# Odd layer's attention: the memory branch runs first, and the compressed branch is computed for all heads between its steps

## The chip, the core and the metric

One NeuronCore of a Trainium2 chip runs the whole program. Its engines have queues of their own: TensorE (PE; its weight loads stand as PEld), VectorE (DVE), ScalarE (ACT), GpSimd (POOL) and SyncE (SP), which here only issues DMAs. They meet at semaphores. TensorE writes to the eight banks of PSUM (`ps`), 128 partitions by 512 fp32 numbers each. The metric is the time of one launch on the device in microseconds (us). All numbers are fp32; one fp32 matmul of this kernel appears in the trace as two MATMUL instructions, a transpose as one.

## What is computed

Two blocks in a row on 512 tokens of width 1024. The change lies in one stage of the odd layer of the first block. That layer's attention, cut to what matters:

```python
def block(s0):                       # queries s0 .. of 12 heads, 2 groups of keys
    sc = jnp.einsum('bghqd,bgjd->bghqj', qb, kcmp) + head_bias(rel_c)      # 31 compressed keys
    pc = masked_softmax(sc, rel_c >= 0) * (tpos >= CMP_BLOCK - 1)...
    oc = jnp.einsum('bghqj,bgjd->bghqd', pc, vcmp)
    ...                              # selected blocks: all 8 blocks of 64 keys are selected
    ps = masked_softmax(ss, (rel_s >= 0)[:, :, None])
    osel = jnp.einsum('bghqk,bgqkd->bghqd', ps, vg)
    ...
    ow = jnp.einsum('bghqk,bgkd->bghqd', pw, vwb)                          # window of 512 keys
    return gb[:, 0, ..., None] * oc + gb[:, 1, ..., None] * osel + gb[:, 2, ..., None] * ow

def odd_layer(...):
    c = nsa_attention(q, kc, vc, ks, vs, kw, vw, gl, ...)
    m = mem_attention(xq, mem_n, w_mem_kv)                                 # 4 heads, 256 memory rows
    y = jnp.concatenate([c, m], axis=-1) * jax.nn.silu(gate)
    return h + (y @ w_out).astype(h.dtype)
```

So a head's output is a gated sum of three branches (compressed, selected, window), and beside the 12 heads stand 4 heads of attention over the memory. Everything goes into `y`, which already holds the gate.

## The kernel before

The program is a list of stages (`STAGES`). After each one `end_phase` (L202) joins all engines at a barrier, so nothing of one stage overlaps the next. The stage of this case is `nsa` (L1455). `compress` (L1351) ahead of it makes the 31 compressed keys `k.kcmpT` and values `k.vcmp` and writes the position bias, one row of 2048 numbers for each head, to `k.bias_dram`. `odd_out` (`out_projection`, L1179) follows it; its first DMA issues (L404, L1205) wait for the barrier.

Queries are in 4 tiles of 128. `nsa` has three parts, one after the other:

1. **The compressed softmax of all heads and tiles** (the prelude). SyncE issues 32 DMAs of bias into `pc` (L1487). TensorE makes the scores, 48 matmuls of a 128-column weight tile on 31 keys (L1502), a head to a bank. VectorE waits for all 32 DMAs and adds them (L1575, one head at a time), then handles all 1488 numbers of a partition at once: minimum (L1579), subtraction (L1585), sum (L1587), gate over sum (L1588, L1589), product (L1590); ScalarE's exponential (L1550) stands between. Scores are negated, so the minimum is the softmax's maximum.
2. **The main loop**, 48 steps (12 heads by 4 tiles t, head by head) in a software pipeline. A tile t has (t + 1) x 128 keys. At iteration u TensorE makes two score banks of step u, selected and window (L1513), then the products of step u-3 (L1524, then the compressed one, L1526), then transposes of step u-2: the compressed weights (L1535), then the two branches (L1541). VectorE adds the bias and takes the minimum of step u (L1601, a custom instruction and its small accumulator read), copies the transposed weights of step u-2 out of PSUM (L1610 the compressed 31 rows, L1612 the window branch) and finishes step u-3 (L1617 to L1628: two small ones, then selected, window and compressed product added up in `acc`, then times `y`). ScalarE takes the exponentials of step u (L1559) and copies the selected branch's transposed weights of step u-2 (L1567). Scores alternate between banks 0, 1 and 2, 3, transposes use banks 4 and 5, products banks 6 and 7.
3. **The memory branch**, `MemAttention` (L915): 16 steps (4 heads by 4 tiles) pipelined likewise. A step is one score matmul (L936), two transposes (L944), two product matmuls (L954) on TensorE; minimum (L975), copy (L981), reciprocal (L987) and scaling (L989) on VectorE; one exponential (L965) on ScalarE. It uses banks 0 to 5 and starts when the main loop's last result is stored.

`k.link` makes VectorE wait for its own instruction to end before the next starts. The order on each engine is the order in which the code issues; no scheduler moves anything.

## Time and profile before

| what | value |
|---|---|
| median of 3 runs | 2745.45 us (2738.14 to 2745.59) |
| the profiled execution | 2748.92 us, its span 2747.0 us |
| TensorE busy, of the span | 2320.9 us, 84% |
| VectorE, ScalarE busy | 823.9 us, 457.9 us |
| `nsa`, first instruction to last | 858.9 to 1099.0 us of the span |

The profiled execution took 3.5 us more than the median, and 1.9 us lie outside its span. In the rows further down a time is counted from the start of the span. The granted clock is the share of TensorE's full 2.4 GHz: 1.00 is 2.4 GHz, 0.50 is 1.2 GHz. A duration in the timeline includes the tail of an instruction, so neighbours on one engine overlap a little; start to start is what an instruction takes in a row of them. A row "x4" is four of a kind in a row, with the time from the first one's start to the last one's end.

### The profile page before, as it was taken

Reading aid. Unit: us, or ns where it says so; the run is one execution under the profiler, and the core shown is the slowest. Engines: PE = TensorE matmul, PEld = TensorE weight load, DVE = VectorE, ACT = ScalarE, POOL = GpSimd, SP = SyncE. Lnnn points to the kernel's source line nnn. Section 1 sums busy time; section 2 is a strip of 40 time slices with the busy share of each in tenths; the row PEclk is TensorE's granted clock in tenths of the full one; section 3 lists DMA queues with packets and bytes.
Section 4 is the critical chain, followed back from the end, with each engine's and each line's share of the span. In section 5 each row is a group of like instructions: output and inputs, shape, how many; then the busy total and the mean of one; then the engine's idle time right before and its main releaser. Section 6 shows DMA issues by size and latency. Waiting matters only on the chain. (4 is left out here: it accounts for less than half of the span.)

```text
span 2747.0 us, 32370 instructions
## 1 busy us (share of the span) xinstructions
PE 2320.9 (84%) x13640; PEld 1728.8 (63%) x13640; DVE 823.9 (30%) x1709; ACT 457.9 (17%) x791; POOL 165.7 (6%) x108
## 2 busy tenths in 40 slices
PE   7999978799976998959947993998989989898882
PEld 5788767678865777748844443656555666566651
DVE  6353164233211787433251215111111111111102
ACT  2222213121310443231201003000000000000001
POOL 0710000000000000730000001000000000000001
PEclk9999999899985999989978996999999999999996
DMA  9443203223332000425162142799999999999994
GB/s 280 140 133 97 72 1 128 88 92 93 106 117 52 17 20 5 168 78 164 59 139 94 61 167 92 320 425 426 426 426 425 427 425 426 425 426 426 426 426 152
DMA packets 148149, 581.70 MB, mean 212 GB/s; under 512 B 34678, under 2 KB 56950, under 8 KB 114038
## 3 DMA queue, kind: packets, MB, share of 16 engines
q1 hardware_dynamic: 143027, 558.59, 52.9%
q0 software_dynamic: 3824, 16.81, 1.7%
q10 hardware_dynamic: 1152, 4.19, 0.4%
q8 instruction: 111, 1.82, 0.3%
q14 instruction: 35, 0.29, 0.0%
HBM read 541.93 MB, written 37.63 MB: 211 GB/s over the span
## 5 line engine op out<-in xcount | busy, mean ns | idle before, releaser
L447 PE MATMUL ps<-w_parts,u_parts 128*128 128x512 f32 (+3 forms) x2016 | 424.2, 372 | 10.1 <-DVE w_parts L416 10.1
L2369 PE MATMUL ps<-mem,mem_u 128*64 128x256 f32 x2880 | 364.4, 409 | 72.9 <-DMA mem<-in_expert_w_gate 70.6
L447 PEld LDWEIGHTS ps<-w_parts,u_parts 128*128 128x128 f32 x2016 | 364.1, 190 | 67.6 <-issue 11.2
L2369 PEld LDWEIGHTS ps<-mem,mem_u 128*64 128x64 f32 x2880 | 254.6, 148 | 181.0 <-issue 93.2
L416 DVE TENSOR_TENSOR w_parts<-w_raw,w_parts 128x2048 fp32r<-128x2048 f32 (+3 forms) x76 | 172.8, 2275 | 407.9 <-ACT w_parts L411 407.9
L2452 DVE TENSOR_TENSOR mem_c<-mem_c,ps 128x256 f32<-128x256 f32 x64 | 26.9, 421 | 763.2 <-issue 702.0
L411 ACT CAST w_parts<-w_raw 128x2048 fp32r<-128x2048 f32 (+3 forms) x76 | 134.8, 1776 | 470.8 <-PE ps L447 209.2
L445 PE MATMUL ps<-u_parts,w_parts 128*128 128x512 f32 x768 | 177.2, 392 | 3.1 <-DVE w_parts L416 3.1
L2369 PE MATMUL ps<-mem_u 128*64 128x256 f32 x1216 | 153.3, 409 | 29.6 <-DMA mem_u<-in_expert_w_gate 28.8
L1227 PE MATMUL ps<-w_parts,u_parts 128*128 128x512 f32 x768 | 175.4, 390 | 0.0
L2382 PE MATMUL ps<-mem,mem_c 128*64 128x512 f32 x736 | 166.8, 592 | 0.5 <-DVE mem_c L2458 0.5
L445 PEld LDWEIGHTS ps<-u_parts,w_parts 128*128 128x128 f32 x768 | 145.2, 189 | 33.5 <-issue 3.4
L1227 PEld LDWEIGHTS ps<-w_parts,u_parts 128*128 128x128 f32 x768 | 144.7, 189 | 29.9
L2361 PE MATMUL ps<-picks,hn_parts 128*128 128x256 f32 x1024 | 140.4, 291 | 19.0 <-DVE picks L2432 19.0
L2361 PEld LDWEIGHTS ps<-picks,hn_parts 128*128 128x128 f32 x1024 | 127.6, 193 | 42.3 <-issue 23.1
L2369 PEld LDWEIGHTS ps<-mem_u 128*64 128x64 f32 x1216 | 106.1, 148 | 75.9 <-issue 39.6
L2422 ACT ACTIVATE mem_c<-ps 128x256 f32<-128x256 f32 x64 | 24.5, 383 | 721.6 <-PE ps L2369 721.6
L2382 PEld LDWEIGHTS ps<-mem,mem_c 128*64 128x64 f32 x736 | 61.2, 137 | 77.6 <-issue 72.5
L2440 DVE COPY mem_u<-ps 128x512 f32<-128x512 f32 x64 | 44.2, 691 | 104.3 <-PE ps L2361 104.3
L1524 PEld LDWEIGHTS ps<-mem_u 128*128 128x128 f32 x480 | 59.0, 191 | 25.6 <-ACT mem_u L1567 14.4
L1524 PE MATMUL ps<-mem_u 128*128 128x128 f32 x480 | 63.5, 279 | 11.4 <-ACT mem_u L1567 9.6
L2416 ACT COPY mem_u<-ps 128x512 f32<-128x512 f32 x64 | 37.5, 585 | 200.3 <-PE ps L2382 200.3
(335 smaller groups left out, 2309.9 us busy)
## 6 DMA issues: line engine op xcount, KB each, us to landing
mem<-in_expert_w_down SPq DMA_DIRECT2D x46, 2048.0 KB, 29.2
mem<-in_expert_w_gate SPq DMA_DIRECT2D x45, 2048.0 KB, 22.4
mem<-in_expert_w_up SPq DMA_DIRECT2D x45, 2048.0 KB, 26.9
mem_u<-in_expert_w_gate SPq DMA_DIRECT2D x19, 2048.0 KB, 22.8
mem_u<-in_expert_w_up SPq DMA_DIRECT2D x19, 2048.0 KB, 27.9
mem_u<-in_expert_w_down SPq DMA_DIRECT2D x18, 2048.0 KB, 29.7
w_raw<-in_od_w_in SPq DMA_DIRECT2D x18, 1024.0 KB, 5.1
ypad<-mem_u SPq DMA_DIRECT2D x128, 128.0 KB, 26.4
```

The costliest lines, as they stand in the source:

```text
L411: act.copy(self.part(n, 0), self.raw(n)).then_inc(self.high, 1)
L416: dve.tensor_tensor(self.part(n, 1), self.raw(n), self.part(n, 0).bitcast(F32), ALU.subtract).then_inc(self.low, 1)
L445: mm = pe.matmul(out, w[x][:, kk, g.t * P:(g.t + 1) * P], u[:, y, ku, :], start=first, stop=last)
L447: mm = pe.matmul(out, u[:, x, ku, g.t * P:(g.t + 1) * P], w[y][:, kk, :], start=first, stop=last)
L1227: mm = pe.matmul(k.ps[:, g.bank, :], parts[g.part // 2][:, x, ky, g.t * P:(g.t + 1) * P], w[z][:, kk, :], start=g.part == 0 and kk == 0 an ...
L1524: pe.matmul(o[:, 128 * i:128 * i + 128], pT[v % 2][:, 512 * i + kt * P:512 * i + kt * P + P], vv[:, kt, g * DH:(g + 1) * DH], start=kt == ...
L2361: mm = pe.matmul(o, k.hn_parts[:, part, m, 2 * r + j, :], k.picks[:, q % 2, m, :, :], start=m + part == 0, stop=m == NT - 1 and part == 1)
L2369: mm = pe.matmul(ps[SLOTS * h:SLOTS * (h + 1), bank, 0:256], x[:, kk, :], w[:, kk, 256 * h:256 * (h + 1)], start=kk == 0, stop=kk == KD - 1)
L2382: mm = pe.matmul(ps[SLOTS * c:SLOTS * (c + 1), ROWS + e % 2, :], aT[:, e % 2, j, SLOTS * h:SLOTS * (h + 1)], w[:, h, j, 512 * c:512 * (c + ...
L2416: act.copy(yn[:, e % STORES, :], ps[:, ROWS + e % 2, :]).then_inc(rows_ready, 1)
L2440: dve.tensor_copy(xT[:, q % 2, 2 * r:2 * r + 2, :], ps[:, GATHER + piece % 2, :] .rearrange("p (j s) -> p j s", j=2)).then_inc(x_ready, 1)
L2452: dve.tensor_tensor(a[:, e % 2, :], sg[:, e % 2, :], ps[:, UP, 0:256], ALU.mult).then_inc(a_ready, 1)
```

## The change

- **Order of the parts.** `ma.tensor`, `ma.scalar`, `ma.vector` (the memory branch) are issued first, the main loop after them. Each of the three takes a function `guest(u)` that issues something ahead of iteration u.
- **The compressed branch as guest.** It is worked on tile by tile, all 12 heads at once. On TensorE the dictionary `c_at` says at which iteration: scores of tile 0 to 3 at 0, 1, 5, 6; transposes ("turn") at 8, 9, 12, 14; products ("mix") at 11, 13, 16, 18. VectorE does `shift(t)` at 4 + t and `scale(t)` at 6 + t, ScalarE the exponentials at 5 + t and the copies out of PSUM. It uses banks 6 and 7 by turns.
- **Four heads per transpose.** A head's 31 weights are padded to 32, so that four heads are one 128 by 128 transpose: 3 of them a tile, 12 in all, where there were 48.
- **Block-diagonal product.** `blocks` holds, for four heads, each head's `vcmp` in its own 32 rows and 128 columns and zeros elsewhere. One matmul of 512 columns gives the product of four heads: 12 in all, where there were 48. GpSimd clears `blocks` (128 by 1536), 12 DMAs put the values in. The results are copied to `y_cmp`.
- **One bias run.** `wide` holds 55 numbers for each head and partition, from which every tile takes 31 at its own offset: 8 DMAs, where there were 32.
- **The main loop** loses the compressed transpose, its copy and its product. VectorE starts the sum from `y_cmp` in the instruction that scales the selected product (now L1713 of the new file), and the separate addition is gone. The wait for `stored` moves from the compressed transpose to the products and is one step looser.
- `load_weights(k, sp, "nsa")` is dropped; at this stage it issues nothing, since the next chunks belong to a stage behind `odd_out`.

The diff, cut (`tensor` and `vector` of the memory branch get `guest` as `scalar` does):

```diff
+    def scalar(self, act, guest=None):
+        for u in range(len(self.steps) + 3):
+            if guest:
+                guest(u)
+            if u >= len(self.steps):
+                continue
             act.wait_ge(self.low, u + 1)
...
+    y_cmp = view(k, RING, NT, NH * DH)
+    blocks = view(k, RING + 6144, N_QUADS, QUAD * DH)
+    wide = view(k, RING + 7680, NH, 56)
+    pcT = view(k, RING + 8352, NT, N_QUADS * P)
...
+    pc = view(k, U0 + 1024, NT, NH, 32)
...
+    c_uses = [("score", t) for t in range(NT)]
+    for at in ("turn", 0), ("turn", 1), ("mix", 0), ("turn", 2), ("mix", 1), ("turn", 3), ("mix", 2), ("mix", 3):
+        c_uses += [at] if at[0] == "turn" else [("mix", at[1], q) for q in range(N_QUADS)]
+    c_at = {("score", 0): 0, ("score", 1): 1, ("score", 2): 5, ("score", 3): 6, ("turn", 0): 8, ("turn", 1): 9,
+            ("mix", 0): 11, ("turn", 2): 12, ("mix", 1): 13, ("turn", 3): 14, ("mix", 2): 16, ("mix", 3): 18}
...
             for a in range(8):
-                for t in range(NT):
-                    src = bass.AP(b.tensor, 1024 + 33 - 8 * t - a, [[64, 16], [2048, NH], [1, NCMP]])
-                    sp.dma_start(pc[16 * a:16 * a + 16, :, t, :], src).then_inc(bc, 16)
+                src = bass.AP(b.tensor, 1024 + 33 - 8 * (NT - 1) - a, [[64, 16], [2048, NH], [1, WIDE]])
+                sp.dma_start(wide[16 * a:16 * a + 16, :, 0:WIDE], src).then_inc(bc, 16)
+            sp.wait_ge(c_cleared, 1)
+            for h in range(NH):
+                i = h % QUAD
+                sp.dma_start(blocks[32 * i:32 * i + NCMP, h // QUAD, DH * i:DH * (i + 1)],
+                             k.vcmp[0:NCMP, h // HPG, :]).then_inc(c_blocks, 16)
             for h in range(NH):
                 if h >= 2:
                     sp.wait_ge(low, 2 * NT * (h - 1))
 
                 src = bass.AP(b.tensor, 2048 * h + 512 - (P - 1), [[1, P], [1, 512]])
                 sp.dma_start(bias_n[:, h % 2, :], src).then_inc(bias_loaded[h % 2], 16)
-            load_weights(k, sp, "nsa")
+
+        @block.gpsimd
+        def _(pool):
+            pool.memset(blocks, 0.0).then_inc(c_cleared, 1)
...
-            for h in range(NH):
-                if h >= 8:
-                    pe.wait_ge(c_biased, h - 7)
-                for t in range(NT):
-                    mm = pe.matmul(k.ps[:, h % 8, NCMP * t:NCMP * t + NCMP], k.qT[:, h, t * P:(t + 1) * P],
-                                   k.kcmpT[:, h // HPG, :], start=True, stop=True)
-                mm.then_inc(c_scored, 1)
-            pe.wait_ge(c_biased, NH)
+            def bank_free(use):
+                i = c_uses.index(use)
+                if i >= 2:
+                    before = c_uses[i - 2]
+                    if before[0] == "score":
+                        pe.wait_ge(c_biased, before[1] + 1)
+                    else:
+                        pe.wait_ge(c_copied, c_number(before))
+
...
+                    t = use[1]
+                    if use[0] == "score":
+                        bank_free(use)
+                        for h in range(NH):
+                            mm = pe.matmul(k.ps[:, c_bank(use), 32 * h:32 * h + NCMP], k.qT[:, h, t * P:(t + 1) * P],
+                                           k.kcmpT[:, h // HPG, :], start=True, stop=True)
+                        mm.then_inc(c_scored, 1)
+                    elif use[0] == "turn":
+                        bank_free(use)
+                        pe.wait_ge(c_ready, t + 1)
+                        for q in range(N_QUADS):
+                            tr = pe.transpose(k.ps[:, c_bank(use), P * q:P * (q + 1)],
+                                              pc[:, t, QUAD * q:QUAD * (q + 1), :].rearrange("p h j -> p (h j)"), k.ident)
+                        tr.then_inc(c_used, 1)
+                    else:
+                        pe.wait_ge(c_copied, c_number(("turn", t)))
+                        if t == 0:
+                            pe.wait_ge(c_blocks, 16 * NH)
+                        for q in range(N_QUADS):
+                            bank_free(("mix", t, q))
+                            pe.matmul(k.ps[:, c_bank(("mix", t, q)), :], pcT[:, t, P * q:P * (q + 1)], blocks[:, q, :],
+                                      start=True, stop=True).then_inc(c_used, 1)
+
+            ma.tensor(pe, guest)
...
+                    if u == 0:
+                        pe.wait_ge(ma.exped, len(ma.steps))
+                    if u == 1:
+                        pe.wait_ge(ma.copied, len(ma.steps))
...
-                    pe.wait_ge(cop_v, 2 * (v + 1))
+                    pe.wait_ge(cop_v, v + 1)
+                    if v == 0:
+                        pe.wait_ge(c_copied, c_number(c_uses[-1]))
+                    if v >= 2:
+                        pe.wait_ge(stored, v - 1)
...
-                    pe.matmul(o[:, 256:384], pT[v % 2][0:NCMP, 1024:1152], k.vcmp[0:NCMP, g, :], start=True,
-                              stop=True).then_inc(mixed, 1)
+                            mm = pe.matmul(o[:, 128 * i:128 * i + 128],
+                                           pT[v % 2][:, 512 * i + kt * P:512 * i + kt * P + P],
+                                           vv[:, kt, g * DH:(g + 1) * DH], start=kt == 0, stop=kt == t)
+                    mm.then_inc(mixed, 1)
...
-                        pe.wait_ge(c_ready, 1)
-                    if v >= 2:
-                        pe.wait_ge(stored, v - 1)
-                    pe.transpose(k.ps[0:NCMP, 6 + v % 2, 384:512], pc[:, h, t, :], k.ident).then_inc(turned, 1)
+                        pe.wait_ge(ma.stored, len(ma.steps))
...
-            pe.wait_ge(stored, n)
-            ma.tensor(pe)
...
-            act.wait_ge(c_shifted, 1)
-            act.activation(pc, pc, ACT.Exp, scale=-1.0).then_inc(c_exped, 1)
+            def guest(u):
+                if 5 <= u < 5 + NT:
+                    t = u - 5
+                    act.wait_ge(c_shifted, t + 1)
+                    act.activation(pc[:, t, :, 0:NCMP], pc[:, t, :, 0:NCMP], ACT.Exp, scale=-1.0).then_inc(c_exped, 1)
...
+                    if use[0] == "turn":
+                        act.wait_ge(c_used, c_number(use))
+                        act.copy(pcT[:, t, :], k.ps[:, c_bank(use), 0:N_QUADS * P]).then_inc(c_copied, 1)
+                    elif use[0] == "mix":
+                        for q in range(N_QUADS):
+                            act.wait_ge(c_used, c_number(("mix", t, q)))
+                            act.copy(y_cmp[:, t, QUAD * DH * q:QUAD * DH * (q + 1)],
+                                     k.ps[:, c_bank(("mix", t, q)), :]).then_inc(c_copied, 1)
...
-            ma.scalar(act)
...
-            dve.wait_ge(bc, 16 * 32)
-            for h in range(NH):
-                dve.wait_ge(c_scored, h + 1)
-                dve.tensor_tensor(pc[:, h, :, :], pc[:, h, :, :],
-                                  k.ps[:, h % 8, 0:NT * NCMP].rearrange("p (t j) -> p t j", t=NT),
-                                  ALU.add).then_inc(c_biased, 1)
-            dve.wait_ge(c_biased, NH)
...
-            dve.tensor_tensor(rows, rows, by_row(c_low), ALU.subtract).then_inc(c_shifted, 1)
-            dve.wait_ge(c_exped, 1)
...
-            dve.tensor_tensor(rows, rows, by_row(c_low), ALU.mult).then_inc(c_ready, 1)
+            def shift(t):
+                x = pc[:, t, :, 0:NCMP]
+                if t == 0:
+                    dve.wait_ge(bc, 16 * 8)
+                dve.wait_ge(c_scored, t + 1)
+                o = 8 * (NT - 1 - t)
+                dve.tensor_tensor(x, wide[:, :, o:o + NCMP], k.ps[:, 6 + t % 2, 0:NH * 32].rearrange(
+                    "p (h j) -> p h j", h=NH)[:, :, 0:NCMP], ALU.add).then_inc(c_biased, 1)
+                dve.wait_ge(c_biased, t + 1)
+                k.link(dve, dve.tensor_reduce(c_low[:, t, :], x, AX_X, ALU.min))
+                dve.tensor_tensor(x, x, spread(c_low[:, t, :], 2, NCMP), ALU.subtract).then_inc(c_shifted, 1)
+
+            def scale(t):
+                x = pc[:, t, :, 0:NCMP]
+                dve.wait_ge(c_exped, t + 1)
+                k.link(dve, dve.tensor_reduce(c_sum[:, t, :], x, AX_X, ALU.add))
+                k.link(dve, dve.reciprocal(c_inv[:, t, :], c_sum[:, t, :]))
+                k.link(dve, dve.tensor_tensor(c_low[:, t, :], c_inv[:, t, :], k.gsig[:, t, 0:NH], ALU.mult))
+                dve.tensor_tensor(x, x, spread(c_low[:, t, :], 2, NCMP), ALU.mult).then_inc(c_ready, 1)
+
+            def guest(u):
+                if 4 <= u < 4 + NT:
+                    shift(u - 4)
+                if 6 <= u < 6 + NT:
+                    scale(u - 6)
+
+            k.link(dve, dve.memset(pc[:, :, :, NCMP:32], 0.0))
+            ma.vector(dve, guest)
...
-                    dve.wait_ge(turned, 3 * v + 1)
-                    dve.tensor_copy(pT[v % 2][0:NCMP, 1024:1152], k.ps[0:NCMP, 6 + v % 2, 384:512]).then_inc(cop_v, 1)
-                    dve.wait_ge(turned, 3 * v + 3)
+                    dve.wait_ge(turned, 2 * v + 2)
                     dve.tensor_copy(pT[v % 2][:, 512:512 + w], k.ps[:, 5, 0:w]).then_inc(cop_v, 1)
...
-                    k.link(dve, dve.tensor_scalar(a, o[:, 0:128], s[:, 3, 0:1], None, ALU.mult))
+                    k.link(dve, dve.scalar_tensor_tensor(out=a, in0=o[:, 0:128], scalar=s[:, 3, 0:1],
+                                                         in1=y_cmp[:, t, h * DH:(h + 1) * DH], op0=ALU.mult, op1=ALU.add))
                     k.link(dve, dve.scalar_tensor_tensor(out=a, in0=o[:, 128:256], scalar=s[:, 3, 1:2], in1=a,
                                                          op0=ALU.mult, op1=ALU.add))
-                    k.link(dve, dve.tensor_tensor(a, a, o[:, 256:384], ALU.add))
                     dve.tensor_tensor(ys, ys, a, ALU.mult).then_inc(stored, 1)
-            ma.vector(dve)
```

How the instructions stand. TensorE at the start of the stage, before: the 48 compressed scores in one run, then the main loop's first scores and turns.

```order
L1502 MATMUL ps<-mem_u 128x31 x48
L1513 MATMUL ps<-mem_u 128x128 x2
L1513 MATMUL ps<-mem_u 128x256 x2
L1513 MATMUL ps<-mem_u 128x384 x2
L1535 MATMUL ps<-mem_c,mem_u 31x128
L1541 MATMUL ps<-mem_c,mem_u 128x128 x2
```

The same place after, iterations 0 to 5 of the memory branch (L938, L946, L956 are its scores, transposes and products; L1547 a group of compressed scores):

```order
L1547 MATMUL ps<-mem_u 128x31 x12
L938 MATMUL ps<-mem_u 128x256
L1547 MATMUL ps<-mem_u 128x31 x12
L938 MATMUL ps<-mem_u 128x256 x2
L946 MATMUL ps<-mem_c 128x128 x2
L938 MATMUL ps<-mem_u 128x256
L946 MATMUL ps<-mem_c 128x128 x2
L956 MATMUL ps<-mem_u,mem_c 128x128 x2
...
L1547 MATMUL ps<-mem_u 128x31 x12
```

The run of 48 is cut into four groups of 12 that stand between steps of the memory branch; that branch came behind the main loop before.

VectorE in the main loop, one iteration, before (L1601 shows as ISA: the custom instruction and its accumulator read, for each of two banks):

```order
L1601 ISA mem<-ps,mem_u 128x256
L1601 ISA mem 128x1
...
L1610 COPY mem_u<-ps 31x128
L1612 COPY mem_u<-ps 128x512
L1617 RECIPROCAL mem<-mem 128x2
L1618 TENSOR_TENSOR mem<-mem,mem_u 128x2
L1624 TENSOR_SCALAR mem_u<-ps,mem 128x128
L1625 SCALAR_TENSOR_TENSOR mem_u<-ps,mem,mem_u 128x128
L1627 TENSOR_TENSOR mem_u<-mem_u,ps 128x128
L1628 TENSOR_TENSOR mem<-mem,mem_u 128x128
```

The same iteration after (L1690 is the old L1601, L1699 the old L1612):

```order
L1690 ISA mem<-ps,mem_u 128x256
L1690 ISA mem 128x1
...
L1699 COPY mem_u<-ps 128x512
L1704 RECIPROCAL mem<-mem 128x2
L1705 TENSOR_TENSOR mem<-mem,mem_u 128x2
L1713 SCALAR_TENSOR_TENSOR mem_u<-ps,mem 128x128
L1715 SCALAR_TENSOR_TENSOR mem_u<-ps,mem,mem_u 128x128
L1717 TENSOR_TENSOR mem<-mem,mem_u 128x128
```

The small copy and one addition are gone, the first scaling now reads a second operand; nothing else moved.

TensorE in the main loop, before, one iteration with a tile of four key blocks in the products:

```order
L1513 MATMUL ps<-mem_u 128x384 x2
L1524 MATMUL ps<-mem_u 128x128 x8
L1526 MATMUL ps<-mem_u 128x128
L1535 MATMUL ps<-mem_c,mem_u 31x128
L1541 MATMUL ps<-mem_c,mem_u 128x128 x2
```

After:

```order
L1578 MATMUL ps<-mem_u 128x384 x2
L1593 MATMUL ps<-mem_u 128x128 x8
L1607 MATMUL ps<-mem_c,mem_u 128x128 x2
```

The compressed product and transpose, which stood between the products and the two branches' transposes, are gone from the loop.

## Rows read from the trace of the kernel before

**Rows 1.** Busy time by stretch: prelude, main loop, memory branch (stretch, length, engines, PEclk)

```profile
858.90:893.50 34.60, 23.80 (x104) 22.66 (x104) 10.13 (x18) 2.73 (x2) 0.00 (x0) 0.50 0.22 38
893.50:1075.60 182.10, 168.56 (x1048) 131.55 (x1048) 146.11 (x577) 73.90 (x240) 0.00 (x0) 0.98 0.06 16
1075.60:1099.00 23.40, 21.70 (x128) 18.52 (x128) 18.55 (x65) 8.94 (x32) 0.00 (x0) 0.85 0.00 1
```

**Rows 2.** Timeline of the prelude (start, duration, engine, line, instruction, [idle before <-releaser])

```profile
858.92 16.40 SPq L1487 DMA_DIRECT2D mem_u<-bias  x32
858.97 13.84 PE L1502 MATMUL ps<-mem_u 128*128 128x31 f32 x64 [1.42 <-PEq L205]
876.76 1.64 DVE L1575 TENSOR_TENSOR mem_u<-mem_u,ps 128x124 f32<-128x124 f32 x8 [18.89 <-DMA mem_u<-bias]
```

**Rows 3.** Timeline of one cycle of four main-loop steps, the chain through it

```profile
946.64 1.16 PE L1524 MATMUL ps<-mem_u 128*128 128x128 f32 x8 [0.84 <-ACT mem_u L1567]
947.73 0.48 PE L1526 MATMUL ps<-mem_u 31*128 31x128 f32 x2
948.28 0.82 PE L1541 MATMUL ps<-mem_c,mem 128*128 128x128 f32 x6
949.13 0.56 DVE L1612 COPY mem_u<-ps 128x384 f32<-128x384 f32 x1 [0.31 <-PE ps L1541]
950.76 0.29 DVE L1627 TENSOR_TENSOR mem_u<-mem_u,ps 128x128 f32<-128x128 f32 x1
951.08 0.29 DVE L1628 TENSOR_TENSOR mem<-mem,mem_u 128x128 f32<-128x128 f32 x1
952.96 0.69 DVE L1612 COPY mem_u<-ps 128x512 f32<-128x512 f32 x1 [0.53 <-PE ps L1541]
955.93 0.48 PE L1526 MATMUL ps<-mem_u 31*128 31x128 f32 x2
956.48 0.38 PE L1541 MATMUL ps<-mem_c,mem_u 128*128 128x128 f32 x2
956.70 1.88 PE L1513 MATMUL ps<-mem_u 128*128 128x512 f32 x4
956.96 0.27 DVE L1612 COPY mem_u<-ps 128x128 f32<-128x128 f32 x1
958.83 0.68 DVE L1601 CUSTOM_DVE_ANT_0 mem_u<-ps,mem_u 128x512 f32<-128x512 f32 x1
961.38 1.16 PE L1524 MATMUL ps<-mem_u 128*128 128x128 f32 x8 [0.84 <-ACT mem_u L1567]
```

**Rows 4.** Groups of the main loop that the change takes out (busy, mean ns | idle before)

```profile
L1627 DVE TENSOR_TENSOR mem_u<-mem_u,ps 128x128 f32<-128x128 f32 x48 | 13.8, 287 | 1.6
L1610 DVE COPY mem_u<-ps 31x128 f32<-31x128 f32 x48 | 13.3, 278 | 13.5 <-PE ps L1535 7.4 <-PE ps L1541 5.0
```

**Rows 5.** Timeline of the memory branch: two products at either clock, a step apart

```profile
1080.23 1.06 PE L954 MATMUL ps<-mem_u,mem_c 128*128 128x128 f32 x4
1082.37 1.06 PE L954 MATMUL ps<-mem_u,mem_c 128*128 128x128 f32 x4
...
1092.80 0.61 PE L954 MATMUL ps<-mem_u,mem_c 128*128 128x128 f32 x4
1093.90 0.61 PE L954 MATMUL ps<-mem_u,mem_c 128*128 128x128 f32 x4
```

**Rows 6.** VectorE's and GpSimd's work of the prelude's kinds, by form

```profile
L1575 DVE TENSOR_TENSOR mem_u<-mem_u,ps 128x124 f32<-128x124 f32 x12 | 2.8, 278 | 23.8 <-DMA mem_u<-bias 18.9 <-PE ps L1502 4.9
L1579 DVE TENSOR_REDUCE mem_u<-mem_u 128x48 f32<-128x1488 f32 x1 | 1.7, 1702 | 0.0
L637 POOL MEMSET mem_u<- 128x1024 f32 x1 | 1.0, 951 | 0.3 <-POOLq L2718 0.3
```

**Rows 7.** Busy time and granted clock (PEclk) where the clock rose or fell

```profile
894.00:899.00 5.00, 4.88 (x9) 2.67 (x10) 2.27 (x12) 3.31 (x13) 0.00 (x0) 0.50 0.00 0
1077.00:1083.00 6.00, 5.48 (x19) 4.62 (x20) 3.36 (x9) 2.42 (x9) 0.00 (x0) 0.50 0.00 0
```

55 lines of the change are left out of this document (33 added, 22 removed).

## The prediction

> **What bounds the kernel now.** I read four views, in this order. The list of stages comes first: barriers part them, so the question is only how long `nsa` takes, and what it gains the program gains. Then the busy times by stretch [rows 1]: the prelude takes 34.6 us, the main loop 182.1, the memory branch 23.4, together 240.1. The reader is to see that the prelude has TensorE at the low clock level (0.50) and VectorE idle most of the time, and that no engine is full in the loop: TensorE 168.6 busy of 182.1, VectorE 146.1. So the third view is the prelude's timeline [rows 2]: all of VectorE's work waits for bias DMAs. SyncE issues 32 of them in 16.40 us, 0.51 each, and VectorE starts at 876.76, 1.4 us after the last issue. The fourth is the timeline of one loop cycle, since with TensorE and VectorE both nearly full the cycle is set by a chain that goes to and fro. From the products at 946.64 to the same ones at 961.38 is 14.74 us, and twelve such cycles are 176.9 of the loop's 182.1. The chain [rows 3]: (a) products, transposes, VectorE's copy of 384 columns, 946.64 to 949.13, 2.49; (b) from that copy to the next, which waited for TensorE, 3.83; (c) from there to the copy of 128 columns, 4.00; (d) from there through a finish to the 512-wide scores at 958.83, 1.87; (e) those scores, two exponentials and a copy on ScalarE, to the products that waited for that copy, 2.55. Sum 14.74.
>
> **The main loop, part by part.** *TensorE loses the compressed product and transpose.* From L1526's start to L1541's is 0.55 in both places shown (947.73 to 948.28, 955.93 to 956.48) [rows 3]. Stretches (a) and (b) end in a wait for TensorE, and their TensorE part contains this once each. In (c) VectorE's copy at 956.96 starts 0.10 us after TensorE's transposes end (956.48 plus 0.38), so TensorE sets this one too, once VectorE is faster. Gain 0.55 each in (a), (b), (c). *VectorE loses an addition,* 0.32 from start to start (950.76 to 951.08) [rows 3]; 48 of them are 13.8 us busy [rows 4]. Only in (d) is it on the chain: gain 0.32. In (b) and (c) it goes beside TensorE's 0.55: VectorE comes earlier and waits for TensorE, which is late next. *VectorE loses the 31-row copy,* 278 ns x 48 [rows 4]; half of its cover is already a wait (13.5 us idle before it), so it adds nothing on the chain where TensorE is awaited. *(e)* keeps its 2.55: none of its operations changes. Cycle after: 1.94 + 3.28 + 3.45 + 1.55 + 2.55 = 12.77, a gain of 1.97, over twelve cycles 23.6 us. Bounds: 1.2 us a cycle (14) if (c) keeps its time and half of (b)'s gain is lost to the scores before it; from above 3 us a cycle (36), where only TensorE's own work is left (168.6 / 12 less 4 x 0.55 is 11.9). I take the chain's 23.6, since it adds up to the measured cycle. *The start.* The loop opens today at the low level: 894 to 899 TensorE is busy 4.88 of 5.00 us at 0.50 [rows 7]. Afterwards it comes behind dense work, and this costs half: gain 2.4. Loop: 26.0. The replaced scaling instruction (two operands instead of one) is costed at nothing: the next one in the loop has that form and both stand in the cycle as it is.
>
> **The front.** Today 34.6 + 23.4 = 58.0 us [rows 1]. Afterwards, from 858.9 on:
> - Iterations 0 and 1: 12 compressed scores are 24 instructions. 64 took 13.84 us at 0.50 [rows 2], so a group takes 5.2, and a memory score some 0.9 more. 12.2 us, to 871.1. VectorE has nothing to do meanwhile.
> - Iterations 2 to 4: a memory step took 2.14 at 0.50 and 1.10 at 1.00 [rows 5]. Three, without the first product: 5.5, to 876.6.
> - Iterations 5 to 9: TensorE at the low level has two more groups (10.4), five steps (10.7) and six transposes (1.3), 22.4 us; at the full level 11.2. VectorE has the whole softmax: per tile five instructions on 372 numbers. Between 124 numbers at 278 ns and 1488 at 1702 [rows 6] a straight line gives 0.54 each; with two small ones at 0.2 that is 3.1 a tile, 12.4 in all. Its memory steps take 18.55 / 16 = 1.16 [rows 1], five are 5.8: 18.2 us. So 18.2 to 22.4; I take 20.5, because the clock will hardly be up while VectorE starves TensorE. To 897.1.
> - Iterations 10 to 18: six steps at the full level 6.6, three last part-steps 1.5, and four product groups. Four 512-wide instructions took 1.88 [rows 3]; a group is six, 2.7, all four 10.8. ScalarE's three copies a group stand ahead of its exponential, and VectorE behind that: 0.4 each, 1.6. Sum 20.5, to 917.6.
>
> The front takes 58.7 us: what the DMA wait and the prelude's idle time gave back, the guests take again. Loss 0.7.
>
> **The Trainium skill against it.** 124 numbers take VectorE 278 ns and 1488 take 1702 [rows 6]: more than in proportion for the small one, so cutting the 1488-wide instructions into quarters is not free. The Trainium skill, page "VectorE: DVE Perf Modes", section "The TRN2 errata", says that instructions on SBUF operands pay a fixed latency each, and advises 512 elements or more; that speaks against tiles of 372. The rows agree. In proportion 372 would take 0.43 and not 0.54, so the rule is worth 16 x 0.11 = 1.8 us of the front, on an engine that sets iterations 5 to 9; with it the front is 58.7, without it 56.9.
>
> **Costs put at nothing.** SyncE's queue: 8 bias DMAs (4.1 us by 0.51 each), then a wait for GpSimd's clear (1536 columns by 951 ns for 1024: 1.4 us [rows 6]), then 12 loads of `blocks` (6.2). With 1.5 to land, the bias is there at 864.5 and the blocks at 871, and the main loop's two bias tables, which now queue behind them, some 3 us later. They are wanted at about 876, 900 and 917; the cover is 11 us or more each. If it were gone, each microsecond late would count in full. The main loop's new waits for the memory branch (exponentials, copies, results) are for work issued ahead of it on every engine, and cost only the drain of the last step, under 1 us, inside the range. The looser wait for `stored` can only help.
>
> **Sum.** 26.0 less 0.7 is 25.3 us. Against the profiled execution: 2748.92 to 2723.6. That execution is 3.5 above the median of 2745.45, so the forecast in the median's terms is 2720.
>
> **Rivals.** About 0.3% (8.2 us) is what a measurement of this kernel can tell from no change.
> 1. *The clock comes up early in the front.* Then iterations 0 to 4 take 8.8 instead of 17.7 us and 5 to 9 take 18.2: the front is 47.5, gain 10.5 more. Against it: in the prelude TensorE ran these 31-column scores for 13.84 us without a pause [rows 2] and the level stayed 0.50 [rows 1]. Time 2709, chance 0.15.
> 2. *The clock stays low through the whole front.* For it: it rose only after 5 to 6 us of dense work in both places of [rows 7], and here runs of such work are cut by guests and waits. Iterations 10 to 18 then take about 37 and 5 to 9 take 22.4: the front is 77, 19 us more than today. 26.0 less 19 leaves 7: 2738, chance 0.12.
> 3. *A wait takes the place of what is removed.* ScalarE's chain (e) or the score matmuls, 1.88 us for a 512-wide set [rows 3], end later than the shortened parts, and the loop gives half, 12 us. Time 2732, chance 0.11. Against it: the chain's five parts add up to the cycle with no rest.
> 4. *Slower.* The low level lasts into the loop. Place: its first cycles. TensorE's 11.9 us of work a cycle become 24, 11 more than 12.8. After case 2 there are 7 us of gain left, so less than one low cycle eats it, and two cycles give 2745.45 - 7 + 22, about 2760. Against it: [rows 1] shows 0.98 over the whole loop though it opens at 0.50. Chance 0.04.
>
> **How the numbers follow.** The forecast of 2720 has 0.58. Faster: forecast and rivals 1 and 3, 0.84. Within 0.3%: rival 2, 0.12. Slower: rival 4, 0.04. The range reaches from rival 1 less a few for the loop's upper bound, 2706, to rival 2, 2738.
>
> **What would show it.** Loop cycle 12.8 (12.0 to 13.6) from one 8-instruction product group to the next; main loop 154 to 159 us; VectorE's first loop score at 912 to 922 of the span; PEclk 0.50 until some 875 at least, up before the loop; the 512-wide block products at 0.9 us a matmul; no wait for a DMA in the stage. Wrong: a cycle above 13.8 (then (b) or (c) has another end), PEclk 0.50 past 910, or a first loop score past 925.

## The result and the profile after

| | before | after |
|---|---|---|
| median of 4 runs each (lowest to highest) | 2745.52 us (2738.14 to 2745.86) | 2715.49 us (2713.24 to 2721.11) |
| ratio after / before, 95% interval | | 0.9895 (0.9882 to 0.9909) |
| profiled execution (span) | 2748.92 us (2747.0) | 2713.24 us (2711.4) |
| `nsa`, its first DMA issue to the next stage's | 858.92 to 1100.29 = 241.4 | 855.60 to 1066.10 = 210.5 |
| main loop, first score to last store | 182.1 | 153.4 |
| the rest of the stage | 59.3 | 57.1 |

The kernel is 30.0 us faster in the medians, 35.7 in the profiled executions. The stage alone gives 30.9; of the remaining 4.8, 3.3 were there before the stage began (858.92 against 855.60), and 1.4 came behind it; the change touches neither part, and in the runs below, too, the stage begins anywhere from 855.60 to 859.05. Stage lengths are therefore compared below, inside one execution each.

Busy time by stretch after, which answers to [rows 1] (stretch, its length, busy time of PE, PEld, DVE, ACT, POOL, then the granted clock, DMA share and GB/s). The first four rows are the front, the last is the main loop with the drain ahead of it:

```profile
855.60:866.40 10.80, 10.76 (x50) 10.61 (x51) 0.52 (x2) 1.85 (x3) 1.37 (x1) 0.52 0.18 42
866.40:871.60 5.20, 5.20 (x23) 3.99 (x23) 2.90 (x8) 1.70 (x6) 0.00 (x0) 0.69 0.51 97
871.60:890.60 19.00, 13.99 (x103) 12.42 (x103) 18.13 (x53) 5.74 (x18) 0.00 (x0) 0.99 0.02 7
890.60:909.00 18.40, 18.40 (x82) 11.38 (x80) 8.28 (x29) 9.92 (x24) 0.00 (x0) 0.92 0.00 1
909.00:1064.80 155.80, 138.64 (x920) 113.25 (x918) 121.87 (x482) 74.65 (x243) 0.00 (x0) 1.00 0.07 18
```

The front is to be read row by row: who is full in each? First TensorE at the low level (0.52; 0.50 means 1.2 GHz) with 31-column scores and VectorE idle (0.52 of 10.80); then VectorE with the softmax (18.13 of 19.00) while TensorE idles 5.0; then TensorE with the block products (18.40 of 18.40) while VectorE is busy 8.28. The work is no longer one after the other as before, but each engine still has its own stretch.

SyncE's queue after, against the 16.40 us of 32 issues in [rows 2]:

```profile
855.60 4.76 SPq L1511 DMA_DIRECT2D mem<-bias  x8
860.40 7.40 SPq L1515 DMA_DIRECT2D mem<-mem_u  x12
867.85 161.78 SPq L1522 DMA_DIRECT2D mem_u<-bias  x12
```

One steady cycle of the main loop after, from VectorE's timeline, only its copies (L1699, the old L1612) and the 512-wide scores (L1690, the old L1601), against [rows 3]:

```profile
982.20 0.56 DVE L1699 COPY mem_u<-ps 128x384 f32<-128x384 f32 x1 [1.05 <-PE ps L1607]
...
985.42 0.69 DVE L1699 COPY mem_u<-ps 128x512 f32<-128x512 f32 x1 [0.60 <-PE ps L1607]
...
988.71 0.29 DVE L1699 COPY mem_u<-ps 128x128 f32<-128x128 f32 x1 [0.29 <-PE ps L1607]
...
990.29 0.69 DVE L1690 CUSTOM_DVE_ANT_0 mem_u<-ps,mem_u 128x512 f32<-128x512 f32 x1
...
994.76 0.56 DVE L1699 COPY mem_u<-ps 128x384 f32<-128x384 f32 x1 [1.05 <-PE ps L1607]
```

From copy to copy: (b) 3.22, (c) 3.29, (d) 1.58, and from the 512-wide scores to the next 384-wide copy, which is (e) and (a), 4.47. Sum 12.56; nine cycles in a row agree within 0.02. The words in brackets say that VectorE now waits for TensorE (L1607, the transposes) ahead of three of its four copies.

What ends (e) is on ScalarE and TensorE, in the same cycle:

```profile
991.02 0.72 ACT L1640 ACTIVATE mem_u<-mem_u,mem 128x512 f32<-128x512 f32 x1 [1.58 <-DVE mem L1690]
...
991.74 0.70 ACT L1640 ACTIVATE mem_u<-mem_u,mem 128x512 f32<-128x512 f32 x1
...
992.44 0.35 ACT L1648 COPY mem_u<-ps 128x256 f32<-128x256 f32 x1
...
992.85 1.16 PE L1593 MATMUL ps<-mem_u 128*128 128x128 f32 x8 [1.19 <-ACT mem_u L1648]
```

The products wait 1.19 us for a copy of what TensorE had transposed by 991.21 (a row at 990.61, 0.60 long); it stands in ScalarE's queue behind two exponentials.

### The profile page after: what moved, and what is told of

Read it like the earlier page. It is cut to its first block and busy times, and to the rows that moved or that the text cites. A ratio compares the mean times of both kernels' runs of the same rounds, so it can differ in the third digit from the quotient of the medians.

```text
span 2711.4 us, 32087 instructions
## 1 busy us (share of the span) xinstructions
PE 2286.1 (84%) x13532; PEld 1703.0 (63%) x13532; DVE 801.2 (30%) x1624; ACT 465.9 (17%) x810; POOL 168.2 (6%) x109
## 3 DMA queue, kind: packets, MB, share of 16 engines
q10 hardware_dynamic: 1152, 4.19, 0.4%
## 5 line engine op out<-in xcount | busy, mean ns | idle before, releaser
L447 PE MATMUL ps<-w_parts,u_parts 128*128 128x512 f32 (+3 forms) x2016 | 423.6, 371 | 11.8 <-DVE w_parts L416 11.8
L2457 PE MATMUL ps<-mem,mem_u 128*64 128x256 f32 x2880 | 356.3, 403 | 64.3 <-DMA mem<-in_expert_w_gate 63.8
L2457 PE MATMUL ps<-mem_u 128*64 128x256 f32 x1216 | 159.6, 421 | 37.2 <-DMA mem_u<-in_expert_w_gate 36.3
L2721 POOL DMA_INDIRECT mem<-ypad,mem_u x8 | 8.5, 1064 | 1025.5 <-PEq L2716 1023.4
```

Source lines behind the costliest of these rows:

```text
L447: mm = pe.matmul(out, u[:, x, ku, g.t * P:(g.t + 1) * P], w[y][:, kk, :], start=first, stop=last)
L2457: mm = pe.matmul(ps[SLOTS * h:SLOTS * (h + 1), bank, 0:256], x[:, kk, :], w[:, kk, 256 * h:256 * (h + 1)], start=kk == 0, stop=kk == KD - 1)
```

## The experiments

All lengths in the tables come from each run's own profile, one execution each. "Front" is the stage's first issue to VectorE's first score of the main loop, "loop" from there to the last store.

These runs also show how far a front can be trusted, since six of the kernels share the front of the changed kernel, one of them with other bias issues. In four of them (addition back, TensorE's two back, and the two built on it) the granted clock came up 14.1 us into the stage, as in the changed kernel itself, and the front took 55.74 to 55.76. In the other two it came up later: in e7 (another order on ScalarE in the main loop) 16.4 us in, and the front took 55.13; in e3 (the bias in 32 DMAs) 16.3 us in, and it took 55.63. So a difference between fronts of less than some 0.6 us shows nothing, and neither does a level that comes up 2.3 us sooner or later.

### What each removed operation was worth in the loop

Four kernels put back, one upon the other, what the change took out of the 48 steps. The work put back is the old kind at the old place; where it would compute nothing new its result is not used.

```diff
 # e4: the addition, VectorE
-dve.scalar_tensor_tensor(out=a, in0=o[:, 0:128], scalar=s[:, 3, 0:1], in1=y_cmp[...], op0=ALU.mult, op1=ALU.add)
+dve.tensor_scalar(a, o[:, 0:128], s[:, 3, 0:1], None, ALU.mult)
 ...
+dve.tensor_tensor(a, a, y_cmp[:, t, h * DH:(h + 1) * DH], ALU.add)
 # e6: product and transpose, TensorE
+pe.matmul(o[:, 256:384], pT[v % 2][0:NCMP, 0:128], k.vcmp[0:NCMP, g, :], start=True, stop=True)
+if v >= 2: pe.wait_ge(stored, v - 1)
+pe.transpose(k.ps[0:NCMP, 6 + v % 2, 384:512], pc[:, t, h, 0:NCMP], k.ident)
 # e56: e6 and VectorE's copy of the 31 rows
+dve.wait_ge(turned_c, v + 1)
+dve.tensor_copy(spare, k.ps[0:NCMP, 6 + v % 2, 384:512])
```

> The changed kernel with VectorE's separate addition of the compressed branch put back into the main loop (one more instruction for each of the 48 steps; the sum is the same). Chain theory: it lies on the path only in stretch (d), so a cycle of four steps goes from 12.56 to about 12.9 us (+0.32) and the main loop from 153.4 to about 157.3 us (+3.9). Rival, VectorE's own sum sets the loop: 4 x 0.32 a cycle, cycle 13.8, loop 168.8 (+15.4).

> The changed kernel with TensorE's 31-row product and 31-column transpose put back into each of the 48 main-loop steps (their results are not used; the old wait for the stored result ahead of the transpose is back too). Chain theory: 0.55 us in each of (a), (b) and (c), cycle 12.56 to about 14.2 us, loop 153.4 to about 173 (+19.8). Rival, TensorE's idle time in the cycle (12.56 less 138.6/12 = 1.0 us) swallows part of it: 4 x 0.55 less 1.0, cycle 13.8, loop about 167 (+14). Second rival, it was the looser wait for the results or VectorE that gave the gain: loop under 160.

> As the run with TensorE's product and transpose back, and VectorE's copy of the 31 transposed rows back too (48 more VectorE instructions of 278 ns; it copies to a place that nothing reads). Chain theory: VectorE waits for TensorE there anyway, so no more than 0.1 us a cycle, within 1.5 us of the run without the copy. Rival, VectorE's sum counts: 4 x 0.28 a cycle, +13 us on that run.

> All three put back: product and transpose on TensorE, copy and addition on VectorE. Chain theory: the cycle is the old one, 14.6 to 14.74 us, the loop 177 to 180 us, of 182.1 before; what is left is the opening at the low clock. Rival, part of the gain came from something else in the change (the new buffer places, the looser waits): the cycle stays below 14.3, loop below 174.

| | (b) | (c) | (d) | (e) + (a) | cycle | loop |
|---|---|---|---|---|---|---|
| before | 3.83 | 4.00 | 1.87 | 5.04 | 14.74 | 182.1 |
| after | 3.22 | 3.29 | 1.58 | 4.47 | 12.56 | 153.4 |
| addition back | 3.21 | 3.41 | 1.90 | 4.48 | 13.00 | 160.1 |
| TensorE's two back | 3.85 | 3.94 | 1.57 | 5.12 | 14.48 | 176.5 |
| and the copy | 3.78 | 3.99 | 1.56 | 5.04 | 14.38 | 175.3 |
| and the addition | 3.79 | 3.99 | 1.88 | 5.04 | 14.70 | 179.1 |

The cycle with TensorE's product and transpose back, VectorE's copies (L1704 here) and scores (L1695), as above:

```profile
993.46 0.56 DVE L1704 COPY mem_u<-ps 128x384 f32<-128x384 f32 x1 [1.24 <-PE ps L1612]
...
997.31 0.69 DVE L1704 COPY mem_u<-ps 128x512 f32<-128x512 f32 x1 [1.24 <-PE ps L1612]
...
1001.25 0.29 DVE L1704 COPY mem_u<-ps 128x128 f32<-128x128 f32 x1 [0.92 <-PE ps L1612]
...
1002.82 0.68 DVE L1695 CUSTOM_DVE_ANT_0 mem_u<-ps,mem_u 128x512 f32<-128x512 f32 x1
...
1007.94 0.56 DVE L1704 COPY mem_u<-ps 128x384 f32<-128x384 f32 x1 [1.24 <-PE ps L1612]
```

Against the rows of after, each of the three stretches that end in a wait for TensorE is longer by 0.63 to 0.65 and (d), which does not, is unchanged (1.57). That is the pattern the chain asks for; the size is a little over the 0.55 of its reading. The rival that TensorE's idle time swallows part (cycle 13.8) fails: TensorE has idle time in the cycle, but not ahead of these operations. The run also puts the old wait for the stored result back, but no row ahead of the transposes (L1606) shows idle time, so in the cycle it is TensorE's work that costs.

The addition alone, the same view:

```profile
986.98 0.56 DVE L1699 COPY mem_u<-ps 128x384 f32<-128x384 f32 x1 [0.72 <-PE ps L1607]
...
990.19 0.69 DVE L1699 COPY mem_u<-ps 128x512 f32<-128x512 f32 x1 [0.27 <-PE ps L1607]
...
993.60 0.29 DVE L1699 COPY mem_u<-ps 128x128 f32<-128x128 f32 x1
...
995.50 0.68 DVE L1690 CUSTOM_DVE_ANT_0 mem_u<-ps,mem_u 128x512 f32<-128x512 f32 x1
```

Read the brackets: with 0.32 more work the wait shrinks from 1.05 to 0.72 and from 0.60 to 0.27, and the stretches keep their length. Ahead of the 128-wide copy there were only 0.29, so the bracket is gone and (c) grows, by 0.12; in (d) the whole 0.32 counts. So 0.44 a cycle, some 5 us over twelve, not the 0.32 and 3.9 expected, and far from the 1.28 of the rival that VectorE's sum sets the loop. The loop is 6.7 us longer, but 1.4 of that belongs to one cycle near its end (14.39 us), in which the clock fell:

```profile
1063.60:1067.00 3.40, 3.01 (x14) 2.61 (x13) 0.83 (x3) 0.48 (x1) 0.00 (x0) 0.50 0.00 0
```

The copy costs nothing: the cycle is even 0.10 shorter with it, which stays unexplained. All three together give 14.70, the old cycle but for 0.04. What the loop then still has ahead of before, 3.0 us, is mostly its opening: from the first score to the first copy of 384 columns it takes 8.88 us instead of 11.35, with the clock up instead of at 0.50. So the new buffer places, which stay in this run, are worth no more than the 0.04. The looser wait and the exchanged scaling instruction are put back here together with the rest; what settles them are the rows: no idle time ahead of the old transposes, and 0.35 us for the scaling in either form.

### What the front's parts are worth

> The kernel before, with one change alone: the memory branch comes first, then the prelude and the main loop as they were (32 bias DMAs, scores in eight banks, one wide softmax). Theory: the DMAs are then hidden by the memory branch, and prelude and memory branch take about 45 to 47 us instead of 58 (the 18.9 us that VectorE waited go, less the 13.8 us of scores at the low level or about 7 at the full one, which it now hides no more). Rival, the front is set by TensorE at the low clock level through the memory branch and the scores: 34 + 14 + 12, about 58 to 60, no gain.

> The changed kernel with the compressed branch not between the steps of the memory branch but as a whole ahead of it (same instructions, same order among themselves). Theory: while VectorE does the softmax TensorE idles and while TensorE does block products VectorE idles, so the front gets longer by 5 to 10 us: from 57.1 to about 62 to 67. Rival, interleaving gives nothing, since each engine's own work adds up either way: within 2 us.

> The changed kernel with its bias in 32 DMAs of three heads each instead of 8 of twelve (same bytes, same place). Theory: 24 more issues of 0.51 to 0.6 us; the last lands at about 874 to 876 instead of 862, and VectorE wants it at 871.0, so the first tile of the softmax is 3 to 5 us late and the main loop begins 0 to 4 us later; then the memory branch hides most of the old DMA wait even without the fewer DMAs. Rival, the queue sets the front: 12 us or more later.

> The changed kernel with the first two groups of compressed scores at iterations 2 and 3 of the memory branch instead of 0 and 1. Theory: the memory steps are dense work for TensorE and bring its clock up before the 31-column scores, so PEclk rises at about 862 instead of 869 and the main loop begins 3 to 5 us earlier. Rival, the clock level has nothing to do with the order: within 1 us.

```diff
 # e1: the kernel before, memory branch first (ScalarE, VectorE alike)
+ma.tensor(pe)
+pe.wait_ge(ma.stored, len(ma.steps))
 for h in range(NH):
 ...
-ma.tensor(pe)
 # e2: the changed kernel (ScalarE, VectorE alike)
-ma.tensor(pe, guest)
+for u in range(19): guest(u)
+ma.tensor(pe)
 # e3: the changed kernel
+for h in range(0, NH, 3):
+    src = bass.AP(b.tensor, 2048 * h + ..., [[64, 16], [2048, 3], [1, WIDE]])
+    sp.dma_start(wide[16 * a:16 * a + 16, h:h + 3, 0:WIDE], src).then_inc(bc, 16)
 # e8: the changed kernel
-c_at = {("score", 0): 0, ("score", 1): 1, ...
+c_at = {("score", 0): 2, ("score", 1): 3, ...
```

| | front | loop | whole stage |
|---|---|---|---|
| before (prelude + memory branch to the end of the stage) | 59.3 | 182.1 | 241.4 |
| after | 55.75 | 153.4 | 210.5 |
| e1, memory branch first, nothing else | 49.2 | 182.2 | 232.8 |
| e2, guests ahead instead of between | 59.2 | 153.2 | 213.7 |
| e3, bias in 32 DMAs | 55.6 | 153.4 | 210.3 |
| e8, scores two iterations later | 54.95 | 153.4 | 209.7 |

**The DMA count is worth little.** With 32 smaller issues (15.64 us of SyncE's queue) the first addition of the bias came 0.38 us late:

```profile
874.58 0.54 DVE L1659 TENSOR_TENSOR mem_u<-mem,ps 128x372 f32<-128x372 f32 x1 [0.38 <-DMA mem<-bias]
```

The 3 to 5 us expected compared the last landing (874.56, as expected) with 871.0, the time at which VectorE wants the bias in the changed kernel's span. In this execution the stage began 2.1 us later and the level came up 2.3 us later into it, so VectorE got there at 874.2. Counted from the stage's start the last bias lands at 16.9 us; it is wanted at 15.4 in the changed kernel and at 16.4 in e7, so 0.5 to 1.5 us late by an estimate from these rows. The front is the same within 0.1 us, which is inside the scatter.

**Moving the memory branch alone saves 8.6 us of the stage,** less than the 12 expected, and leaves a front 6.5 us *shorter* than that of the whole change. So the compressed branch as it is now done costs the front more than it did, 6.5 us, and gets that back more than four times over in the loop. Why less than 12: the clock, as far as these rows go. Busy times by stretch of this run (memory branch; scores; scores; softmax):

```profile
860.00:877.00 17.00, 16.36 (x119) 14.44 (x117) 15.97 (x60) 7.47 (x28) 0.00 (x0) 1.00 0.39 72
877.00:880.00 3.00, 2.63 (x24) 2.63 (x24) 0.88 (x3) 0.00 (x0) 0.00 (x0) 1.00 0.00 0
881.00:896.00 15.00, 14.62 (x70) 14.49 (x69) 2.58 (x10) 0.00 (x0) 0.00 (x0) 0.50 0.00 0
896.00:905.00 9.00, 2.91 (x8) 2.00 (x8) 7.35 (x6) 1.44 (x1) 0.00 (x0) 0.50 0.00 0
```

With the memory branch the level came up to 1.00, and it fell 2.7 us into the 31-column scores (877.37 to 880.1); the 15 us from 881 on have it at 0.50 although TensorE is busy 14.62 of 15.00. All 96 instructions took 18.23 us. At the full level they would take some 11, an estimate from the groups of 24 at 2.76 us each in e11; the 7 us between the two are more than what the run fell short of.

**Interleaving as such is worth 3.4 us,** less than expected (5 to 10), more than the rival's 2. Part of it is the clock: with the guests ahead, all four score groups follow each other at the low level, which lasts 27.8 us into the stage. The first 20 us:

```profile
856.00:876.00 20.00, 20.00 (x97) 20.00 (x97) 6.28 (x13) 2.55 (x4) 1.10 (x1) 0.50 0.25 53
```

**Scores two iterations later gained 0.8 us, not 3 to 5.** That is inside the rival's 1 us, and most of it is scatter: against e7, where the level came up at the same time, the front is 0.2 us shorter. The level did not come up at about 862 but 16.4 us after the stage began (14.1 in the changed kernel, 16.4 in e7 with the order unchanged). The scores began before it was up:

```profile
857.90:873.90 16.00, 15.98 (x66) 14.98 (x67) 2.86 (x9) 3.53 (x9) 1.36 (x1) 0.50 0.29 62
```

In e7, with the changed kernel's order, the same stretch of the stage:

```profile
858.79:875.10 16.31, 16.26 (x66) 15.03 (x67) 2.94 (x9) 3.54 (x9) 1.37 (x1) 0.50 0.29 61
```

### Two reasons turned into changes

Two readings say what still costs time: the copy behind the exponentials in (e), and the stretches of the front with one engine idle and the clock low. Each was tried.

```diff
 # e7: ScalarE, main loop; half(v) is the copy of the old order
+first = u < n and steps[u][1] == NT - 1
+if first: half(u - 2)
 if u < n: ... two exponentials ...
-if u >= 2: ... copy ...
+if u >= 2 and not first: half(u - 2)
 # e9: the table
-c_at = {scores 0, 1, 5, 6; turns 8, 9, 12, 14; mixes 11, 13, 16, 18}
+c_at = {scores 3, 5, 7, 9; turns 10, 12, 14, 16; mixes 11, 13, 15, 17}
+shift_at, exp_at, scale_at = [5, 7, 9, 11], [7, 9, 11, 13], [9, 11, 13, 15]
 # e10: both.   e11: e10 and
+c_at = {scores 4, 6, 8, 10; turns 11, 13, 15, 17; mixes 12, 14, 16, 18}
+shift_at, exp_at, scale_at = [6, 8, 10, 12], [8, 10, 12, 14], [10, 12, 14, 16]
+first = 2 <= u < n and steps[u][1] in (0, NT - 1)
```

> The changed kernel with one order turned round on ScalarE in the main loop: in the iterations with 512-wide scores (one in four) the copy of the transposed block stands ahead of the two exponentials instead of behind them. Theory: in stretch (e) TensorE's products wait 1.05 to 1.4 us for that copy, which was ready to run but stood behind two exponentials of 0.7 us; the cycle goes from 12.56 to 11.6 to 12.0 us, the loop from 153.4 to 142 to 147 us. Rival, the exponentials come later by the copy and the next transposes wait for them instead: cycle 12.4 to 12.7.

> The changed kernel with another table for the compressed branch: its score groups at iterations 3, 5, 7 and 9 of the memory branch, and the steps of the softmax, transposes and block products two iterations apart behind them, in tile order. Theory: the memory branch's first steps bring TensorE's clock up before the first 31-column scores (with the memory branch alone in front the level rose at 859.3, 3.5 us after the stage began), and VectorE and TensorE work beside each other all through; from the stage's first issue to the first loop score 55.75 us become 47 to 50. Rival, the scores bring the level down again (with memory branch and prelude apart it fell 3 us into them): 54 us or more.

> Both edits: copy first, and the spread table. Theory: they lie in different parts of the stage and add up; front 47 to 50 us, loop 142 to 147 us, 13 to 20 us less than the changed kernel, about 2693 to 2702 us. Rival, one of the two gives nothing: 2704 to 2710 us.

> The run with both edits, with two more: every entry of the table one iteration later (scores at 4, 6, 8, 10, the rest as far behind them as the ends allow), and ScalarE's copy first also in the iterations with 128-wide scores. Front, theory: with scores at 3 the first group began at 862.49, 3.9 us after the stage did, and the level stayed low to 871; the memory branch alone had its level up 3.5 to 4 us after the start, so one more dense iteration gets it up before the scores, and the first group (5.17 us at the low level, 2.76 at the full) and three memory steps (2.1 against 1.1 each) take half: front 44 to 46.5 us instead of 49.84. Rival, the scores bring it down again or it stays low: 49 us or more. Loop, theory: the copy of 384 columns stands behind two 128-wide exponentials and TensorE waits 0.55 for it, 0.3 to 0.4 of which goes: cycle 11.99 to about 11.65, loop 146.7 to 142 to 144. Rival, the exponentials come later and something waits for them: cycle 11.9 to 12.1.

| | front | (b) | (c) | (d) | (e) + (a) | cycle | stage | median (runs) | ratio to before, 95% |
|---|---|---|---|---|---|---|---|---|---|
| after | 55.75 | 3.22 | 3.29 | 1.58 | 4.47 | 12.56 | 210.5 | 2715.49 (4) | 0.9895 (0.9882 to 0.9909) |
| e7 | 55.1 | 3.50 | 3.30 | 1.57 | 3.63 | 11.99 | 203.2 | 2707.75 (4) | 0.9865 (0.9850 to 0.9880) |
| e9 | 49.87 | | | | | 12.56 | 204.6 | 2711.78 (1) | |
| e10 | 49.84 | | | | | 11.99 | 197.9 | 2699.96 (5) | 0.9840 (0.9824 to 0.9856) |
| e11 | 46.27 | 3.21 | 3.30 | 1.57 | 3.63 | 11.72 | 191.3 | 2700.20 (5) | 0.9834 (0.9815 to 0.9853) |

**Copy first (e7)** takes 0.84 off (e) + (a) and gives 0.28 of it back in (b). VectorE's copies show where:

```profile
981.45 0.56 DVE L1705 COPY mem_u<-ps 128x384 f32<-128x384 f32 x1 [0.20 <-PE ps L1607]
...
984.95 0.69 DVE L1705 COPY mem_u<-ps 128x512 f32<-128x512 f32 x1 [0.89 <-PE ps L1607]
```

The bracket ahead of the 512-wide copy grew from 0.60 to 0.89: TensorE came later there, because the next ScalarE copy (384 columns) stood behind two 128-wide exponentials, which until then had been over in time. Turning that order round too (e11) brings (b) back to 3.21 and the cycle to 11.72, as expected (11.65). e11 therefore confirms both which order it was and that the exponentials had slack.

**Spread guests (e9)** shorten the front by 5.9 us, inside what was expected, but for one of its two reasons only: the level came up 13.0 us after the start, in e9 as in e10, not the 3.5 expected (3.8 in e1). The first group began at 862.49 of e10's span, and at 5.17 us it ran at the low level. One iteration later (e11) the first group and those behind it look like this, in TensorE's timeline:

```profile
862.57 1.06 PE L956 MATMUL ps<-mem_u,mem_c 128*128 128x128 f32 x4
863.42 2.88 PE L1548 MATMUL ps<-mem_u 128*128 128x31 f32 x24
866.14 0.68 PE L938 MATMUL ps<-mem_u 128*128 128x256 f32 x2
866.65 0.38 PE L946 MATMUL ps<-mem_c 128*128 128x128 f32 x2
866.87 0.61 PE L956 MATMUL ps<-mem_u,mem_c 128*128 128x128 f32 x4
```

The level came up 6.2 us into the stage, at 863.7. The same 24 instructions take 2.88 instead of 5.17, the steps behind them 1.1 instead of 2.1, and the level stays up through all four groups with memory steps between them:

```profile
857.50:863.40 5.90, 5.56 (x16) 4.09 (x17) 2.65 (x7) 3.46 (x9) 1.30 (x1) 0.50 0.28 61
863.50:882.00 18.50, 18.50 (x153) 17.73 (x152) 13.25 (x40) 4.19 (x14) 0.00 (x0) 1.00 0.17 40
882.00:903.70 21.70, 20.45 (x100) 13.12 (x99) 15.05 (x49) 12.96 (x30) 0.00 (x0) 1.00 0.00 1
```

TensorE is now busy 44.51 of 46.10 us, all through, and VectorE beside it. The front is 46.27 us, 9.5 less than in the changed kernel and less than that of e1, which has no block products in it.

The stage of e11 is 6.5 us shorter than e10's, but the medians of the whole program are equal, 2700.20 and 2699.96, with intervals that overlap. In the profiled executions what comes after the stage took 1651.8 us in e11 and 1646.5 in e10. The two stages right behind it take the same in both (287.7 and 287.8 us), so they hand the gain on; the 5.3 us arise later, 3 of them in the stretch that streams weights at 425 GB/s (1700 to 2600). Among all the runs here this rest took 1645.3 to 1651.8 us, and the five runs of each kernel spread over 10 to 13. Only one execution of e11 has a profile, so it is also open whether the level comes up that early each time. Whether the 6.5 us reach the end of the program is not settled by these runs. Both kernels beat the changed one: 0.984 and 0.983 of before against 0.9895, with intervals that don't overlap its own; e10's 2699.96 us lies in the 2693 to 2702 expected.

## Why the prediction was right, point by point

Forecast 2720 us, measured 2715.5; gain 25.3 forecast, 30.9 measured in the stage. The mechanism came as forecast in the loop, where nine tenths of the gain lie; there and in the front the forecast was too low by 2.7 and 2.9 us, so no error hid another. That forecast and median lie only 4.5 us apart is in part luck: the profiled execution, at 2713.24, is 10.4 below the 2723.6 that the prediction gave for it, and 4.8 of these are scatter outside the stage.

1. **Main loop, 26.0 forecast, 28.7 measured.** The chain's parts: (a) was forecast 1.94 and (e) 2.55, together 4.49, measured 4.47; (b) 3.28, measured 3.22; (d) 1.55, measured 1.58; (c) 3.45, measured 3.29. Cycle 12.77 against 12.56. The one term mis-sized is (c): its gain is 0.71, not 0.55. There both engines stand close together (0.10 us between the transposes' end and the copy in [rows 3], 0.29 of wait after), so TensorE's part (0.65 when put back alone) and some of VectorE's addition (0.12) both count; the forecast allowed only the one that was late next. This is worth 0.16 of the 0.21 a cycle, 2 of the 2.5 us that the cycles gained more than forecast.
2. **The costs by operation.** TensorE's two 0.55 a stretch forecast, 0.63 to 0.65 put back alone and 0.56 to 0.70 with VectorE's copy; the addition 0.32, in (d) only, against 0.44 (0.32 upon the others); the 31-row copy nothing, as forecast. The opening 2.4, measured 2.5 with all three put back (8.88 against 11.35 to the first copy of 384 columns).
3. **Front, 0.7 loss forecast, 2.2 us gain measured.** Iterations 0 and 1 took 11.8 us (12.2 forecast). Iterations 2 to 4 took 4.2 (867.4 to 871.62) instead of 5.5, since the level came up 14.1 us into the stage, not after 16; in e3 and e7, with the same order, it came up 16.3 and 16.4 us in, so which of the two a run meets is chance (their fronts are 0.1 and 0.6 us shorter even so). Iterations 5 to 10 took 19.0 (to 890.64; forecast 20.5 and 1.1 for iteration 10). This is the one step that failed: "the clock will hardly be up while VectorE starves TensorE". It was up (0.99 over that stretch, with TensorE busy 13.99 of 19.00), so VectorE's own 18.2 was the right value, the lower end given for iterations 5 to 9; with 1.16 for iteration 10 it makes 19.4. Iterations 11 to 18 took 20.0 against 19.4: the level fell once, at 890.1, behind the stretch in which TensorE waited for VectorE, and the first block-product group paid for it, 4.19 against 2.83 for the next:

```profile
889.85 0.99 PE L956 MATMUL ps<-mem_u,mem_c 128*128 128x128 f32 x4 [1.25 <-DVE mem_c L989]
890.64 4.19 PE L1563 MATMUL ps<-mem 128*128 128x512 f32 x6
...
897.18 2.83 PE L1563 MATMUL ps<-mem 128*128 128x512 f32 x6
```

4. **The rule on narrow instructions.** The five kinds of steps on 372 numbers took 0.53 to 0.55 us, where the straight line through [rows 6] gave 0.54 and proportion 0.43. The Trainium skill, page "VectorE: DVE Perf Modes", section "The TRN2 errata — SBUF-src ops pay a fixed extra latency per instruction", agrees with that. The 1.8 us put on it are an estimate in a stretch that VectorE does set (18.13 of 19.00); no run here has wider steps between those of the memory branch, so they are not shown.
5. **Costs at nothing.** The last bias landed at 861.95 and was wanted at 871.0, and no wait for a DMA stands in the stage: a cover of 9.1 us, where 11 had been forecast. With 32 issues, which take 10.9 us more of the queue, it was 0.4 us short, so the fewer DMAs, part of the change, bought no more than the 0.4 to 1.5 us above.
6. **Rivals.** Rival 1 (clock early) came true by a small part, 2 us sooner, and in five of seven executions with this order. e11 shows its mechanism: with the level up 6 us into the stage, the front is 46.3; the forecast for that case was 47.5. But e11 has another order as well, and that alone gave 5.9 us (e9), so the two numbers agree in part by chance. Rivals 2 and 4 did not come; the 0.50 of e2's first 20 us and of e1's scores show that rival 2's mechanism exists. Rival 3 had the right place, ScalarE's chain (e), but not the result: (e) is 2.56 after and 2.55 before, so it takes nothing back; it is merely the part of the cycle that the change left.

Of the signs named, these came: cycle 12.56 (12.0 to 13.6), first loop score 55.75 us after the stage's start (53 to 63), block products 2.83 a group or 0.94 a matmul (0.9) once the level was up, no wait for a DMA. Two were missed by a little: the loop took 153.4 (154 to 159), and the level was to stay at 0.50 until 16 us into the stage and came up 14.1 us in.

## What to carry to other kernels

Where two engines hand work to and fro, write down the cycle from wait to wait and cost each edit only in the stretches that end in a wait for its engine; here this gave 12.77 for 12.56, and putting the operations back one by one gave the same stretches. A second engine that is only 0.1 to 0.3 us earlier counts too: take both. When work is moved into another loop, the order of its pieces is worth trying by itself (front 55.75, 49.9 or 46.3 us for the same instructions, in one profiled execution each), and a copy that someone waits for belongs ahead of exponentials that nobody does.
